# A hybrid decoder layer on eight cores: the next tile's input prepared inside the last stage, and work ordered by function table

## The reference, cut to what matters

```
h = x + 0.5 * rms_norm(swiglu(rms_norm(x, ng[0]), f1_gate, f1_up, f1_down), ng[1])
mix = token_mixer(rms_norm(h, ng[2]), ...)        # GLA linear attention beside a short gated convolution
h = h + rms_norm(mix, ng[3])
h = h + 0.5 * rms_norm(swiglu(rms_norm(h, ng[4]), f2_gate, f2_up, f2_down), ng[5])
gate = sigmoid(rms_norm(h, ng[6]) @ w_ple_gate)
h = h + rms_norm((p @ w_ple_proj) * gate, ng[7])
```

## Time and profile before

| | us |
|---|---|
| median of 3 runs (lowest to highest) | 1738.25 (1724.28 to 1743.67) |
| profiled execution, its own time | 1734.09 |
| its span, slowest core (core 3) | 1732.6 |
| spans of the eight cores | 1695.8 to 1732.6 |
| TensorE busy on core 3 | 1578.7 (91%) |
| ACT busy / DVE busy | 774.3 / 661.6 |

### The profile page before, as it was taken

The page is one execution under the profiler, slowest core; times in us unless marked ns, Lnnn a source line. Parts: engine busy times, 40 slices in busy tenths (PEclk is TensorE's granted clock), DMA queues, the critical chain, the costliest instruction groups (busy, mean ns, idle before and its releaser), DMA issues.

```text
span 1732.6 us, 27888 instructions; the slowest of 8 cores (1695.8 to 1732.6 us)
## 1 busy us (share of the span) xinstructions
PE 1578.7 (91%) x9405; PEld 1528.4 (88%) x9405; DVE 661.6 (38%) x1301; ACT 774.3 (45%) x1495; POOL 267.0 (15%) x509
## 2 busy tenths in 40 slices
PE   5999999799998799998989999879999998989985
PEld 4999889699997799988878999769998887989984
DVE  0431454433314543055534321454305555333035
ACT  5212664561237721375554114772126565611265
POOL 2211111022111021111111111102111110111110
PEclk9999988789999899999988888889999995999997
DMA  9965743368666798654446655579755453555651
GB/s 238 260 190 176 194 134 102 85 172 231 188 175 164 215 269 244 182 170 134 139 122 196 181 175 149 166 208 284 224 182 172 132 173 97 154 166 178 208 155 66
DMA packets 94541, 305.40 MB, mean 176 GB/s; under 512 B 10770, under 2 KB 31522, under 8 KB 93636
## 3 DMA queue, kind: packets, MB, share of 16 engines
q0 software_dynamic: 72608, 278.33, 56.3%
q1 hardware_dynamic: 21796, 25.29, 5.4%
HBM read 292.83 MB, written 10.75 MB: 175 GB/s over the span
## 4 chain that ended last, share of the span: by engine, by line
PE 75%; ACT 8%; DVE 6%; issue 5%; DMA 5%; SPq 1%; DVEq 0%; ACTq 0%; POOLq 0%
PE ps_bank L457 75%; ACT L488 2%; DMA sb_wring<-f2a 2%; DMA sb_ucx<-x 1%; ACT sb_xnB L488 1%; DVE sb_xnA L491 1%; DVE sb_hA L491 1%; ACT sb_sqA L488 1%; ACT sb_xnA L488 1%; DVE sb_hB L491 1%; DMA sb_wring<-f1b 1%; ACT sb_ta L488 1%; DVE sb_xnB L491 1%; ACT sb_sqB L488 1%; SPq L447 1%
## 5 line engine op out<-in xcount | busy, mean ns | idle before, releaser
L457 PE MATMUL ps_bank<-sb_xnA,sb_wring 128*128 128x344 f32 x2784 | 516.7, 334 | 13.5 <-DMA sb_wring<-f2a 6.4
L457 PE MATMUL ps_bank<-sb_xnB,sb_wring 128*128 128x344 f32 x2784 | 504.3, 330 | 1.6 <-ACT sb_xnB L488 0.9
L457 PEld LDWEIGHTS ps_bank<-sb_xnA,sb_wring 128*128 128x128 f32 x2784 | 474.8, 201 | 21.5 <-issue 21.1
L457 PEld LDWEIGHTS ps_bank<-sb_xnB,sb_wring 128*128 128x128 f32 x2784 | 467.1, 198 | 4.4 <-issue 4.1
L457 PE MATMUL ps_bank<-sb_WB,sb_wring 128*128 128x344 f32 (+1 forms) x1328 | 239.9, 329 | 18.3 <-DVE sb_WB L1000 11.9
L457 PEld LDWEIGHTS ps_bank<-sb_WB,sb_wring 128*128 128x128 f32 x1328 | 223.8, 199 | 21.2 <-issue 21.1
L457 PE MATMUL ps_bank<-sb_WA,sb_wring 128*128 128x344 f32 x1296 | 229.4, 325 | 1.8 <-DMA sb_wring<-f1b 1.2
L457 PEld LDWEIGHTS ps_bank<-sb_WA,sb_wring 128*128 128x128 f32 x1296 | 211.9, 194 | 4.3 <-issue 4.1
L488 ACT ACT_TABLE_LOAD x101 | 129.6, 1283 | 28.3 <-PE ps_bank L457 7.8
L572 POOL DMA_DIRECT2D sb_wring<-f2a x132 | 69.7, 528 | 408.5 <-PE ps_bank L457 383.8
L572 POOL DMA_DIRECT2D sb_wring<-f1a x132 | 69.7, 535 | 315.4 <-PE ps_bank L457 295.5
(11 more groups left out here) (182 smaller groups left out, 1525.0 us busy)
## 6 DMA issues: line engine op xcount, KB each, us to landing
sb_wring<-f1a POOLq DMA_DIRECT2D x132, 512.0 KB, 9.8
sb_wring<-f2a POOLq DMA_DIRECT2D x132, 512.0 KB, 5.2
sb_wring<-f1b POOLq DMA_DIRECT2D x48, 704.0 KB, 5.6
sb_wring<-f2b POOLq DMA_DIRECT2D x48, 704.0 KB, 4.9
sb_wring<-wca POOLq DMA_DIRECT2D x24, 512.0 KB, 8.0
sb_wring<-wo POOLq DMA_DIRECT2D x24, 512.0 KB, 5.5
sb_wring<-wpg POOLq DMA_DIRECT2D x24, 512.0 KB, 7.1
sb_wring<-wg POOLq DMA_DIRECT2D x12, 512.0 KB, 6.2
```

The source lines that it names most:

```text
L457: ins = e.matmul(out.ap, a.ap, b.ap, start=(first and i == 0), stop=(last and i == n_ - 1))
```

## The change

There are two parts. First, `turn` no longer prepares the next tile. POOL loads the next tile's x into chunks 10 to 17 of `W` as the second feed-forward ends (`load_x`, behind the two loads of `p`). In `ple`, behind each of the eight gate products, one chunk is squared by ACT into chunks 18 to 21 of `W` and scaled in place by DVE (`xprep`); the sums of squares go into a PSUM bank that is held through the stage (`bx`), and the factor is made as the stage ends. The next `ffn` reads its operand from `W` (`S.far`) and puts its gated tensor into `xn` and the free chunks of `W` (`hid_slot`). The end of the last stage (`turn` with `leave`) runs inside that `ffn`, behind its first two products, at the lowest priority.

Second, `pick` puts an operation whose table is not the one loaded 4.0 us (by the planner's clock) behind in the comparison. Beside these, the squares of the first two tiles go to DVE, and the load of x into `h` for the residual begins two steps later in the first feed-forward.

```
+LEAVE = -20.0
+SWITCH = 4.0
             t = max(o.due, self.free[o.eng])
-            key = (t if o.due > self.free[o.eng] + 0.15 else self.free[o.eng], o.due - o.prio)
+            tab = o.kw.get("table")
+            turn = SWITCH if tab is not None and tab != self.table else 0.0
+            key = (t + turn if o.due > self.free[o.eng] + 0.15 else self.free[o.eng], o.due - o.prio + turn)
...
         def xv(S, c, n, r=True):
-            return S.xn.v(c * n, (c + 1) * n, r=r)
+            return S.W.v((10 + c) * n, (11 + c) * n, r=r) if S.far else S.xn.v(c * n, (c + 1) * n, r=r)
+
+        def hid_slot(S, j, n):
+            if S.far:
+                if j < 8:
+                    return S.xn.v(j * n, (j + 1) * n, r=True)
+                k = 18 + j - 8 if j < 12 else 8 + j - 12 if j < 14 else j - 14
+            else:
+                k = j
+            return S.W.v(k * n, (k + 1) * n, r=True)
...
+                if j == 1 and S.tail is not None:
+                    yield from S.tail()
+                    S.tail = None
...
+        def load_x(S, T):
+            for c in range(8):
+                dst = S.W.v((10 + c) * T.n, (11 + c) * T.n, r=True)
+                dma_in("pool", "xin%d%s" % (c, S.name), dst, x_src(T, c))
...
-                act(q, hv(S, c, n), AF.Square)
+                tt(q, hv(S, c, n), hv(S, c, n), ALU.mult)
...
             for c in range(8):
-                if N is not None:
-                    enter_chunk(S, N, c, nxt)
-                    if c >= 1:
-                        yield pe([nxt[0]], [S.sb.v(0, S.sb.W)], True)
-                        flush(S, n, nxt, cnt, 8, 1)
...
-                later(leave, -URGE)
-            if N is not None:
-                owner[0] = None
-                yield pe(nxt, [S.sb.v(0, S.sb.W)], True)
-                flush(S, n, nxt, cnt, 8)
-                rsq(S, n, S.rs, eps1)
+                later(leave, LEAVE)
...
+            bx, xq, xseen = None, [], [0]
+            if N is not None:
+                bx = yield from hold()
+            def xprep(c):
+                xr = S.W.v((10 + c) * n, (11 + c) * n)
+                q = S.W.v((18 + c % 4) * n, (19 + c % 4) * n, r=True)
+                act(q, xr, AF.Square)
+                ts(S.W.v((10 + c) * n, (11 + c) * n, r=True), xr, gvec(0, c), None, ALU.mult, None)
+                xq.append(q)
...
+            yield pe(xq, [bx.v(0, n)], True)
+            xsum(0)
+            P.prio = URGE
+            t = ta().v(0, n)
+            act(t, bx.v(0, n), AF.Ln, bias=eps1)
+            act(S.rs.v(0, n), t, AF.Exp, scale=-0.5)
...
+            S.far = True
+            S.tail = lambda: turn(S, T, pend, seen)
```

More of the change, by code:

```diff
@@ L687, in evac @@
             act(q, bank.v(0, n), AF.Square)
-            act(xv(S, m, n), bank.v(0, n), AF.Identity, scale=gvec(g, m, half))
+            act(raw(S, m, n), bank.v(0, n), AF.Identity, scale=gvec(g, m, half))
             pend.append(q)
@@ L700, in ffn @@
             n = T.n
-            hid = lambda j: S.W.v(j * n, (j + 1) * n, r=True)
+            hid = lambda j: hid_slot(S, j, n)
             enter_stage(S, n, 16 * NJ + 176)
             for j in range(NJ):
-                if early is not None and j >= 6 and j < 14:
-                    early(S, T, j - 6)
+                if early is not None and j >= 8 and j < 16:
+                    early(S, T, j - 8)
+                if j == 1 and S.tail is not None:
+                    yield from S.tail()
+                    S.tail = None
                 w = yield from get(S, fA_d[f], j, 1024)
@@ L732, in ffn @@
                     w = yield from get(S, fB_d[f], 2 * m + half)
-                    yield pe([S.W.v(half * 11 * n, (half + 1) * 11 * n), w.all] + (pend if half else []), [bk.v(0, n)])
+                    yield pe([hid(half * 11 + kk) for kk in range(11)] + [w.all] + (pend if half else []), [bk.v(0, n)])
                     if half:
@@ L1193, in enter, with turn @@
             rsq(S, T.n, S.rs, eps1)
-        def turn(S, T, pend, seen, N):
+        def turn(S, T, pend, seen):
             n = T.n
-            nxt, cnt = [], [0]
             yield pe(pend, [S.sb.v(0, n)], True)
@@ L1230, in ple, with xsum @@
             pend, seen = [], [0]
+            bx, xq, xseen = None, [], [0]
+            if N is not None:
+                bx = yield from hold()
+            def xsum(keep):
+                while len(xq) > keep:
+                    mm(bx.v(0, n), [(csr.v(C_OD, C_OD + 128, r=True), xq.pop(0))], xseen[0] == 0, xseen[0] == 7)
+                    xseen[0] += 1
+            def xprep(c):
[4 more added lines that the diff above has]
+                xq.append(q)
             for m in range(8):
[L1232 to L1235, removed]
                 if m % 2 == 0:
@@ L1246, in ple @@
                 flush(S, n, pend, seen, 8, 2)
+                if N is not None:
+                    xsum(2)
+                    xprep(m)
                 yield pe([wp_.all, wv_(S, T, "p", 0, 2 * n)], [bp_.v(0, n)])
@@ L1269, in ple @@
                 later(out)
-            yield from turn(S, T, pend, seen, N)
+            if N is None:
+                yield from turn(S, T, pend, seen)
+                return
+            yield pe(xq, [bx.v(0, n)], True)
[4 more added lines that the diff above has]
+            act(S.rs.v(0, n), t, AF.Exp, scale=-0.5)
+            P.prio = 0.0
+            drop(bx)
+            S.far = True
+            S.tail = lambda: turn(S, T, pend, seen)
         def stream_prog(S, mine):
@@ L1276, in stream_prog, with fetch @@
                 yield from mixer(S, T)
-                yield from ffn(S, T, 1, 5, 6, load_p)
-                yield from ple(S, T, mine[k + 1] if k + 1 < len(mine) else None)
+                N = mine[k + 1] if k + 1 < len(mine) else None
+                def fetch(T=T, N=N):
+                    load_p(S, T)
+                    if N is not None:
+                        load_x(S, N)
+                yield from ffn(S, T, 1, 5, 6, fetch)
+                yield from ple(S, T, N)
         dma_in("sp", "c_ngl", ngl.v(0, 64), ngl_d[:, :])
```

41 lines of the change are left out of this document (15 added, 26 removed).

## The result

| | before | changed |
|---|---|---|
| first comparison, median of 4 runs each (lowest to highest), us | 1731.26 (1721.63 to 1743.67) | 1673.38 (1669.56 to 1675.66) |
| the same pair of kernels on another chip (`changed_2`), 7 and 4 runs | 1711.4 (1709.02 to 1712.89) | 1670.4 (1668.98 to 1672.62) |
| table loads on ACT / products of TensorE | 101 / 9405 | 77 / 9405 |

What follows compares the result with a forecast made beforehand. The turn was taken as bound by loads through four shared buffers, then ACT; mixer passages by table loads. Turns 19, mixers 10 and start 2 made 31 us, from 1738.25 to 1707 us, range 1692 to 1732.

Steps and rivals of the forecast that it cites:

- rival (c): Whole kernel: gapless TensorE draws more spells at clock 0.81, 11.5 us lost per 100 us; up to 1756 us; chance 0.07.
- turns: Between tiles: DMA waits and scale-and-square steps go, saving two thirds of 28.0 us lost, 19 us (8 to 28).
- mixers and second feed-forwards: Passages into and through the mixers: fewer table loads on the chain save two thirds, 10 us (0 to 15).
- start: Before the first product: DVE takes eight squares from ACT, saving 2 us (0 to 3.4).
- DMA queue: Last stage: x stands on POOL's queue ahead of the weights, delay hidden, cost 0; other end 10 us.
- tail in the feed-forward: Next feed-forward: the old tile's end adds 9 us on DVE for each stream, covered there, cost 0.
- At most the smaller number of each pair comes off, 12 loads, 15.4 us: Six mixer passages: upper limit on table loads leaving the chain, of 15 on it; two thirds taken, 10 us.
- rival (a): ACT binds the new turn and the deferral pays for itself: turns 8, mixers 5; 1725 to 1735 us; chance 0.24.
- none in the turns: Turns: of the 20 table changes expected to go, none fall there; 14 loads each, as before.
- Rival (b): More comes than forecast: 15 in mixers, 26 in turns, 3 at start, 44 us; 1694 us; chance 0.13.
- Tables: ACT, whole kernel: 103 planned table changes become 83; loads in the profile near 82, not 101.
- The drain: ACT table switches: the skill page adds about 1.38 us each, 2.66 in all; the trace showed 1.28, so left out.

Runs made afterwards that it cites:

- squares_on_dve: The changed kernel with the 32 squares of the next x made by DVE in place of ACT: 1669.2 us, 0.975 of before.
- The rule alone: The kernel before with only the table rule in `pick` added, x still prepared between the tiles: 1699.44 us against 1714.38, ratio 0.9921.
- x alone: The changed kernel with the table rule switched off, so all the rest of the change: 1703.84 us, 0.9948 of before.
- x_only_2: The repeat on another chip of the changed kernel without the table rule, the run behind x alone: 1703.84 us, 0.9948 of before.

## Why the prediction was wrong

The direction was right, and the mechanism of both parts, but not their independence; the number was 34 us too high: 7 us since the forecast went off a median of 1738.25 where four runs have 1731.26, 17 for the clock and 10 for the sum.

**The base (24 us).** The median was a time of cores at 0.918 to 0.933. The profile showed it: cores 0, 1, 6 and 7 took 1695.8 to 1705.6 us at 0.948 to 0.952, and core 3 1732.6. I had priced such spells at 0.115 us per us, and in rival (c) only let them grow. The slowest of the four undisturbed cores, with the 1.5 us around its span, less 31 would have been 1676. That the changed kernel has fewer slow cores on that chip is measured; whether its order is why, no run settles: on the second chip neither kernel has them in the runs compared, and `squares_on_dve`, nearly the same order, had one execution of four with two cores at 0.911 and 0.915 (1705.91 us).

**The sum (10 us).** Forecast 31, measured 41; the mean spans of undisturbed cores differ by 39:

| term | predicted | measured, means of the second table | the two cores of the first table |
|---|---|---|---|
| turns | 19 (8 to 28) | 15 | 11 |
| mixers and second feed-forwards | 10 (0 to 15) | 18: 22 in the first two, 4 given back in the third | 20: 22 less 2 |
| the end | not in the sum | 6 | 6 |
| start | 2 | 0 (first event at 184.1 and 184.6 us) | 0 |
| DMA queue, tail in the feed-forward | 0 | no wait for `wpg` or `wpp`; the dense stretch at full pace | |

- *Mixers*, the step of the sum that failed: "At most the smaller number of each pair comes off, 12 loads, 15.4 us" was no upper end. 16 loads came off in these columns, and in the first two mixers each was worth 1.8 us and not 1.28, since at the place shown above the idle is shorter and the products behind it run at a higher clock. I had counted loads on one core's chain, not those that hold up the other stream. The rule alone gives 22 us in the first two mixers, loses 8 in the third, and stays inside my range at 13.
- *Turns*: two thirds of 28 was a guess between ends, and 4 us high. The stretch behind B's factor improved as forecast (more than 160 products in 30 us: 190), but 43 products fewer fit ahead of it. This is rival (a)'s point: ACT holds the sums there (2.59 us behind `sb_sqB`), and squares on DVE lift the stretch.
- *Sums of independent terms*: I added tables and turn. In the turns the rule alone gives nothing, x alone 3 us, both 15. Nor was "none in the turns" right: their columns hold 14 loads each before, 16 with x alone and 12 with the rule, so x in the last stage adds two to each and the rule takes four off. With the rule alone the two loads fewer gave no time, since the streams came earlier and the loads of x did not.
- *Rival (b)*, 1694, was nearest by its number, and for a part of its reasons: shorter chains keep the clock up. Its 26 us in the turns and 3 at the start did not come.
- *The end* was overlooked: the diff changes `leave`'s priority for the last tiles too, where there is no cover left but a stage that waits. I had put the cost of the old tile's end at 0 and not asked what it cost before.
- *Tables*: 82 expected, 77 measured. I had silu and tanh as two tables; they share one here. In the changed kernel's trace, silu of A (`sb_tg1A`) follows tanh of B (`sb_tg0B`) with no load:

```profile
548.86 0.49 ACT L494 ACTIVATE sb_tg1B<-sb_tg1B 128x344 f32<-128x344 f32 x1
549.26 0.47 ACT L494 ACTIVATE sb_tg0B<-sb_tg0B 128x344 f32<-128x344 f32 x1
549.64 0.47 ACT L494 ACTIVATE sb_WB<-sb_WB 128x344 fp32r<-128x344 f32 x1
550.44 0.49 ACT L494 ACTIVATE sb_tg1A<-sb_tg1A 128x344 f32<-128x344 f32 x1 [0.33 <-DVE sb_tg1A L497]
```

- *The drain*: by the Trainium skill (ScalarE: Activation LUTs, "What ACT_TABLE_LOAD costs") each switch would take 2.66 us; the trace after has again 1.28 from 216.39 to the exponential at 217.68.
- *DMAs*: the weights of the last stage land later, 10.6 us against 7.1 as the median over each program, and no core of the changed kernel's profiles shows a wait of TensorE for them. The 0 was right.
- *Rival (c)* did not come: spells remain (the digits of 7 and 8 late in the page's clock row, where core 7 loses 13 us on core 0 in the third mixer's column), but in the first profiles there are fewer, and the slowest core's clock rose from 0.918 to 0.935.

## What to carry to other kernels

Take the base of a forecast from a core at the clock that the kernel would have undisturbed, and name the clock's share apart. When two waits stand behind each other at one boundary, price them together: removing either shows the other, and here the rule alone gave the turns nothing, x alone 3 us, and both 15. Where two streams share one engine that loads function tables, a load can cost the other stream's chain as well, and the slower clock after its idle. What a load less is worth depends on what else is waited for, here from 0.3 to 1.8 us: the rule took 22 loads (28 us of ACT) off the kernel before for 14 us of its time, and 24 (31 us) off the kernel with x in the last stage for some 33 (0.9948 to 0.9757).

## What the runs showed of the hardware

- Silu and tanh need no load between them (above). Nor does an exponential behind tanh, here of `x_only_2`, core 0, one reason why the trace before has 101 loads and not the planner's 113:

```profile
555.65 0.49 ACT L494 ACTIVATE sb_tg0A<-sb_tg0A 128x344 f32<-128x344 f32 x1
556.05 0.47 ACT L494 ACTIVATE sb_rsA<-sb_ta 128x344 f32<-128x344 f32 x1
```

- TensorE's clock at 0.81 over 130 us was on core 3 while core 1 of the same die had 1.00, and the slow cores of the first chip came in pairs: 2 and 3, 4 and 5 in the profile of before, 6 and 7 in that of the changed kernel. By the Trainium skill (TensorE: Matmul & The Clock Gate, Part 1) the limiter acts on a whole die; these pairs disagree. On one chip a whole die sat at 0.79 to 0.84 in every execution, which fits it, and there the kernel before took 1804 us.
